# RoPE's half swap from DMA copies to a TensorE permutation, and the weight sums from bf16 to fp32

## The reference

```
h  = modulate(rms_norm(x, g_attn), sh_a, sc_a)
q_w, k_w, v_w, q_n, k_n, v_n, q_g, k_g, v_g = split_mixer_inputs(h @ w_in, qk_g)   # rms norm per head of q and k
q_w, k_w = apply_rope(q_w, cos, sin), apply_rope(k_w, cos, sin)
q_g, k_g = apply_rope(q_g, cos, sin), apply_rope(k_g, cos, sin)

def apply_rope(x, cos, sin):
    x1, x2 = x[..., :half], x[..., half:]
    return concatenate([x1 * cos - x2 * sin, x2 * cos + x1 * sin], axis=-1)
```

## Time and profile before

| what | value |
|---|---|
| median of three runs | 1783.89 us |
| the profiled execution's own time | 1784.84 us |
| its span, first to last instruction | 1783.0 us |
| VectorE / ScalarE / GpSimd busy | 959.8 / 663.4 / 784.2 us |
| dense matmuls (L890), three forms | 581.1 + 378.1 + 310.9 us |
| DMA, mean over the span | 100 GB/s |

### The profile page before, as it was taken

How to read it: one execution, slowest core, us unless ns; L and a number is a source line. 1 busy time by engine, 2 the same in 40 slices (tenths; PEclk the granted TensorE clock), 3 DMA queues, 4 the chain that set the end, 5 groups by cost and what they waited for, 6 DMA issues and landing times.

```text
span 1783.0 us, 27785 instructions
## 1 busy us (share of the span) xinstructions
PE 1665.5 (93%) x10959; PEld 1229.3 (69%) x10959; DVE 959.8 (54%) x1715; ACT 663.4 (37%) x1218; POOL 784.2 (44%) x576
## 2 busy tenths in 40 slices
PE   7999988977989999999899998997887999999998
PEld 3688877866856678666776687886776645645646
DVE  4434498894458851686418844457995612112112
ACT  3222367774243320243013113226875354053130
POOL 2234345652523553345414342551334557468363
PEclk9999999999989999999999998998999899999999
DMA  9355542313124523345225422554003224333332
GB/s 317 48 129 141 131 128 79 90 49 83 36 82 132 149 65 95 95 130 154 59 84 172 148 71 48 144 132 109 16 1 89 78 71 119 94 96 105 83 83 83
DMA packets 317279, 179.11 MB, mean 100 GB/s; under 512 B 88526, under 2 KB 310494, under 8 KB 317150
## 3 DMA queue, kind: packets, MB, share of 16 engines
q1 hardware_dynamic: 284542, 143.63, 30.7%
q10 hardware_dynamic: 32608, 33.71, 6.1%
HBM read 158.97 MB, written 2.83 MB: 91 GB/s over the span
## 4 chain that ended last, share of the span: by engine, by line
PE 60%; DVE 5%; POOL 2%; issue 2%; ACT 2%; SPq 1%; DMA 0%; DVEq 0%; ACTq 0%; POOLq 0%
PE acc L890 55%; PE small L1161 1%; DVE act L1612 1%; DVE stat L1774 1%; DVE prob_t L1788 1%; POOL split_w L656 1%; DVE scaled_ffn L1626 1%; PE side L1071 0%; POOL pair_w L762 0%; PE mod_ps L987 0%; ACT prob_t L1413 0%; DVE o_sum L1800 0%; PE side L880 0%; SPq L546 0%; ACT prob L1391 0%
## 5 line engine op out<-in xcount | busy, mean ns | idle before, releaser
L890 PE MATMUL acc<-act,pair_w 128*128 128x512 f16 x3168 | 581.1, 345 | 6.7 <-ACT act L1277 4.2
L890 PEld LDWEIGHTS acc<-act,pair_w 128*128 128x128 f16 x3168 | 307.6, 98 | 270.1 <-DVE act L1612 9.4
L890 PE MATMUL acc<-act,split_w 128*128 128x512 f32 (+1 forms) x1920 | 378.1, 355 | 9.1 <-DVE act L1874 2.9
L890 PEld LDWEIGHTS acc<-act,split_w 128*128 128x128 f32 x1920 | 307.6, 190 | 61.8 <-DVE act L1874 4.8
L890 PE MATMUL acc<-hidden,split_w 128*128 128x512 f32 (+1 forms) x1584 | 310.9, 358 | 10.6 <-issue 6.3
L890 PEld LDWEIGHTS acc<-hidden,split_w 128*128 128x128 f32 x1584 | 261.3, 189 | 57.7 <-issue 7.1
L653 POOL TENSOR_SCALAR split_w<-raw_w 128x1024 fp32r<-128x1024 f32 (+1 forms) x120 | 126.0, 1050 | 396.3 <-PE acc L890 301.8
L656 POOL TENSOR_TENSOR split_w<-raw_w,split_w 128x1024 fp32r<-128x1024 f32 (+1 forms) x120 | 278.3, 2319 | 10.0
L759 POOL TENSOR_SCALAR pair_raw<-pair_raw,weight_scale 128x1024 f32<-128x1024 f32 x88 | 105.8, 1202 | 356.8 <-ACT pair_w L1462 356.8
L1937 DVE SCALAR_TENSOR_TENSOR mod_acc<-mod_chunk,silu_c,mod_acc 128x256 f32<-128x256 f32 x280 | 228.1, 857 | 4.0
L1637 DVE SCALAR_TENSOR_TENSOR x_t<-acc,mod,x_t 128x512 f32<-128x512 f32 x96 | 60.3, 658 | 254.1 <-PE acc L890 253.6
(11 more groups left out here) (188 smaller groups left out, 1831.8 us busy)
## 6 DMA issues: line engine op xcount, KB each, us to landing
mod_chunk<-in_w_mod ACTq DMA_DIRECT2D x28, 1024.0 KB, 5.4
pair_raw<-in_w_gate SPq DMA_DIRECT2D x44, 512.0 KB, 4.1
pair_raw<-in_w_up SPq DMA_DIRECT2D x44, 512.0 KB, 5.5
raw_w<-in_w_in SPq DMA_DIRECT2D x64, 256.0 KB, 3.7
raw_w<-in_w_down SPq DMA_DIRECT2D x32, 512.0 KB, 3.8
raw_w<-in_w_mod SPq DMA_DIRECT2D x24, 512.0 KB, 4.1
mod_start<-in_w_mod SPq DMA_DIRECT2D x8, 1024.0 KB, 12.1
ks<-q_split SPq DMA_DIRECT2D x64, 96.0 KB, 2.2
```

What stands on the lines that cost most here:

```text
L890: mm = pe.matmul(acc[slot][:, a:b], weights[:, part == 2, k, :], moving[:, part == 1, k, a:b], start=(k == 0 and part == 0), stop=(k == n ...
```

## The change

The swap becomes a matmul. A constant `swap`, 128 by 128 in fp32, with a one at (p, p ^ 32), is loaded with the other constants. A new function `after_norm(j - 3)` stands in TensorE's loop between the dense work of unit j and `after_copy(j - 1)`: it waits for `q_normed`, from the second on also for `q_sin_ready` of the one before, and writes the swapped tile into the PSUM bank `small` by one fp32 matmul of 512 columns. `rotate` reads it there. `swap_halves` and its DMAs are gone, and with them ScalarE's wait for `q_normed` at that place.

`rotate(m - 4)` moves ahead of `take_values` and `inverse` on VectorE. The weight sums use `ones` and `weight_sum` in fp32 instead of the bf16 pair.

```diff
-            for dst, src in ((pair_ones, k_pairs), (cos, k_cos), (sin, k_sin)):
+            for dst, src in ((pair_ones, k_pairs), (swap, k_swap), (cos, k_cos), (sin, k_sin)):
...
-            pool.memset(ones16[:, :], 1.0).then_inc(filled, 1)
...
-                if n == 0:
-                    pe.wait_ge(filled, 3)
...
-                high = weight_sum[:, 2 * f:2 * f + 2].bitcast(BF16)[:, 1:4:2]
-                pe.matmul(mod_ps[:, 0:2], ones16[:, :], high, start=True, stop=True).then_inc(weight_ps, 1)
+                pe.matmul(mod_ps[:, 0:2], ones[:, :], weight_sum[:, 2 * f:2 * f + 2], start=True, stop=True).then_inc(weight_ps, 1)
...
+                def after_norm(j):
+                    if not 0 <= j < 16 or QKV[j][0] not in "qk":
+                        return
+                    i = l * N_ROPE + rope_before(j)
+                    pe.wait_ge(q_normed, l * N_QK + qk_before(j) + 1)
+                    if i >= 1:
+                        pe.wait_ge(q_sin_ready, i)
+                    pe.matmul(small[:, 0:LAT], swap[:, :], q_n[i % 2][:, :], start=True, stop=True).then_inc(q_swapped, 1)
...
+                    after_norm(j - 3)
                     after_copy(j - 1)
...
-                def swap_halves(j):
-                    if not 0 <= j < 16 or QKV[j][0] not in "qk":
-                        return
-                    r = l * N_ROPE + rope_before(j)
-                    sc.wait_ge(q_normed, l * N_QK + qk_before(j) + 1)
-                    if r:
-                        sc.wait_ge(q_ready, r)
-                    for p in range(0, P, 32):
-                        sc.dma_start(q_sin[p:p + 32, :], q_n[r % 2][p ^ 32:(p ^ 32) + 32, :]).then_inc(swap_in, 16)
...
-                    swap_halves(j - 3)
...
-                    ve.wait_ge(swap_in, 64 * (r + 1))
-                    ve.tensor_tensor(q_sin[:, :], q_sin[:, :], sin[:, :], ALU.mult).then_inc(q_sin_ready, 1)
+                    ve.wait_ge(q_swapped, r + 1)
+                    if r:
+                        ve.wait_ge(q_ready, r)
+                    ve.tensor_tensor(q_sin[:, :], small[:, 0:LAT], sin[:, :], ALU.mult).then_inc(q_sin_ready, 1)
...
+                    rotate(m - 4)
+                    take_values(m - 2)
                     inverse(m - 2)
-                    take_values(m - 2)
-                    rotate(m - 4)
...
+    swap = (p[:, None] == (p[None, :] ^ 32)).astype(f)
```

More of the change, by code:

```diff
@@ L206, in trunk @@
 def trunk(nc, x, c, ctx, c_ctx, w_mod, b_mod, norm_attn, norm_ffn, w_in, qk_norm, sink, rpb, w_out,
-          w_gate, w_up, w_down, k_ident, k_pairs, k_cos, k_sin, k_window, k_columns, out):
+          w_gate, w_up, w_down, k_ident, k_pairs, k_swap, k_cos, k_sin, k_window, k_columns, out):
     inv_dram = nc.dram_tensor("inv_rows", [2, 2, TOK], F32, kind="Internal").ap()
@@ L230, in trunk @@
         pair_ones = place("pair_ones", [P, P], F32)
+        swap = place("swap", [P, P], F32)
         ones = place("ones", [P, P], F32)
-        ones16 = place("ones16", [P, P], BF16)
         cos = place("cos", [P, LAT], F32)
@@ L362, in trunk @@
         qkv_copied, q_sq, q_ssq, q_root, q_inv = sem("qkv_copied"), sem("q_sq"), sem("q_ssq"), sem("q_root"), sem("q_inv")
-        q_normed, swap_in, q_cos_ready, q_sin_ready, q_ready = (
-            sem("q_normed"), sem("swap_in"), sem("q_cos_ready"), sem("q_sin_ready"), sem("q_ready"))
+        q_normed, q_swapped, q_cos_ready, q_sin_ready, q_ready = (
+            sem("q_normed"), sem("q_swapped"), sem("q_cos_ready"), sem("q_sin_ready"), sem("q_ready"))
         v_ps, v_ready, v_hi = sem("v_ps"), sem("v_ready"), sem("v_hi")
@@ L1974 @@
 N_VECS = 4 + 3 * DEPTH
-N_CONST = 6
+N_CONST = 7
 def shape_constants():
@@ L1997, in shape_constants @@
         columns[:, VARIANT[cb]] = np.where(ok, 0, NEG)
-    return {"k_ident": ident, "k_pairs": pairs, "k_cos": cos, "k_sin": sin.astype(f),
+    return {"k_ident": ident, "k_pairs": pairs, "k_swap": swap, "k_cos": cos, "k_sin": sin.astype(f),
             "k_window": window, "k_columns": columns}
```

## The result

The changed kernel takes 1798.32 us (median of 5 runs, 1795.54 to 1804.24), the kernel before, timed beside it, 1783.89 (5 runs, 1781.23 to 1788.44). The ratio is 1.0083 with a 95% interval of 1.0057 to 1.0107: slower by 14.8 us, give or take 4.5. I had forecast 1805.2, which is 21.3 us more, with a range of 1797.5 to 1811.0. The ratios of this document leave out three single executions that took far longer than all others (9469.82 us in experiment 2, 1935.27 in experiment 6, 2418.45 of the kernel before beside experiments 5 to 8).

What follows compares the result with a forecast made beforehand. TensorE, busy 93% and full in the projections and gate and up, was taken to bound the kernel. Swaps 14.2, sums 6.6 and waits 0.5 add 21.3 us to 1783.89, giving 1805.2 us, range 1797.5 to 1811 for 8 in 10.

Steps and rivals of the forecast that it cites:

- The swap matmuls: Projections, both layers: 16 fp32 matmuls of 512 columns at 0.89 us, 14.2 us (13.9 to 17.0), on TensorE's path.
- The weight sums: 44 sums, 22 in a layer: fp32 instead of bf16 adds 0.15 us each, 6.6 us (4.0 to 7.9).
- these stand in a stream that is 60.00 of 60.00 busy, so this is on the path too: Weight sums: with TensorE full in gate and up of layer 1, their 6.6 us counts wholly in the time.
- the sums vanish: Rival: fp32 sums vanish between big matmuls, leaving 14.2 + 0.5, 1798.6 us; one part cheap, either one, 0.19.
- The new waits: TensorE waits for normed tiles, units 4 and 6 in layer 1: 0.5 us (0 to 4.8).
- What is free: Projections: dropped copy DMAs, ScalarE's wait, PSUM read, later reciprocal, constant load and attention's start cost or gain nothing.
- The sum: Whole kernel: 14.2 + 6.6 + 0.5 = 21.3 us more, 1805.2 us from the median.
- signs of being right: Swap 0.87 to 0.9 us; projections full, about 7 us longer; VectorE waits for TensorE, not DMA; gate-and-up period 10.5.
- The swap waits in full: Rival: lateness of units 4 and 6 in layer 1 paid fully, 4.8 not 0.5 us, 1809.5; chance 0.14.
- A swap costs one record: Rival: a swap takes one record of 0.435 us, not two, 1798.0 us; one part cheap, either one, 0.19.
- Faster: Rival: VectorE's chain paces the projections, so 44.3 us of waiting come back, 1760.9 us; chance 0.04.
- The clock: Attention's start: later arrival may shift low-clock stretches a few us either way; widens the range, no chance of its own.

Runs made afterwards that it cites:

- experiment 2: Kernel before with only the weight sums in fp32: 1785.7 us, ratio 1.0000 (0.9989 to 1.0012).
- experiment 6: Kernel before with the weight sums in fp32 in layer 0 only: 1784.55 us, ratio 0.9998 (0.9985 to 1.0011).
- experiments 5 to 8: Kernel before with fp32 sums and moved late modulation, fp32 sums layer 0 only, layer 1 only; changed kernel with doubled swap: 1780.76, 1784.55, 1783.82, 1813.82 us.
- experiment 5: Kernel before with late modulation moved off hidden tiles 7 and 15 and weight sums in fp32: 1780.76 us, ratio 0.9978 (0.9965 to 0.9992).
- experiments 1 and 4: Changed kernel with sums back in bf16: 1800.73 us, ratio 1.0089; changed kernel with late modulation moved off the chunk's last tile: 1797.87 us, ratio 1.0068.
- experiment 9: Changed kernel with VectorE's old order (inverse, take_values, then rotate): 1799.91 us, ratio 1.0080 (1.0058 to 1.0101).
- experiment 8: Changed kernel with every swap matmul issued twice: 1813.82 us, ratio 1.0161 (1.0139 to 1.0182).
- experiments 6 and 7: Kernel before with fp32 weight sums in layer 0 only: 1784.55 us, ratio 0.9998; in layer 1 only: 1783.82 us, ratio 1.0000.
- experiment 3: Kernel before with late modulation moved off the chunk's last tile (from tiles 7, 15 to 6, 14): 1777.83 us, ratio 0.9959 (0.9946 to 0.9972).

## Why the prediction came out as it did

**The swap matmuls: right.** Forecast 0.89 us each and 14.2 in all, all of it on the path. Measured 0.86 us between starts, 13.8 in all, 6.80 or 6.94 in layer 0, and 13.74 when doubled. The Trainium skill's Perfetto Trace Analysis, section Engine Utilization, read as the cost of a whole matmul, would have had half of it; the swap runs in two records, each at that rate, and the trace is what decides.

**The weight sums: the step that failed.** Two things are to be told apart. The size: 0.12 us each (0.115 as a stage's mean, 0.92 for 8) and not 0.15, so 5.0 and not 6.6 us gross. I had taken the 0.21 us between starts from a train of squares for a lone sum; the lone one takes 0.14 (1583.67 to 1583.81), against 0.03 in bf16. And the step "these stand in a stream that is 60.00 of 60.00 busy, so this is on the path too". That row is of layer 1. In layer 0 the gate and up units are as full, but the down projections behind them contain pauses that depend on how VectorE stands to GpSimd, and there the 2.3 us come back as 1.20 and, by the execution, 1.72 to 4.20. A stage being full says that its own length grows by the edit, which it did; it does not say that the sum over the stages does. The net price in the kernel before is 0.0 (experiment 2, with 2 us to either side), and 2.9 to 3.4 with the pause gone (experiment 5). My rival "the sums vanish", 1798.6, came nearest to the time and for a reason that was not its own: they don't vanish between the big matmuls, they are paid and given back elsewhere.

**The new waits: too small.** Forecast 0.5 us, bounds 0 and 4.8. The projection of layer 1 is longer by 10.55, 9.49, 10.13 and 9.03 us in four profiles with the swap and the new order (experiments 1 and 4 are the last two), of which 6.8 is the swap itself, so 2.2 to 3.7 remain; but the sums alone and the kernel before again have 1.8 and 2.1 there too, without any swap matmul, so measured from those profiles the change adds only 0.1 to 2.0 beside its 6.8. What is the change's own among these I can bound and not settle: the waits for `q_n` are 1.0 and 1.6 us in two executions, and a clock fall of about 1.6 us stands behind the wait in one of them. The forecast had the mechanism (unit 4's inverse behind SyncE's eight issues) and the place, and priced VectorE's side of it at its undisturbed durations. Unit 6, the larger lateness in its rows, waited 0 us in the first profile of the kernel after and 0.48 in the second.

**What is free: nearly right.** VectorE's wait moved from DMA to TensorE as told, and TensorE waited for nothing there but the tiles of the paragraph above. Turning `rotate` ahead is neither gain nor loss in the time (experiment 9), though it moves the rotation's addition beside GpSimd's split.

**The sum.** Forecast 14.2 + 6.6 + 0.5 = 21.3. With the pause out of the way the chip gives 20.0; 13.8 for the swap and 3.4 for the sums leave 2.8 for waits, with 3 us of uncertainty on the 20.0 and on the 3.4 alike. The forecast's terms are then 0.4 and 3.2 us too high and 2.3 too low, which leaves it 1.3 above the 20.0. In the kernel as it stands it is 14.4, and the 5.6 that are left are the pause and the clock behind it. That the time fell into the range is so partly luck: the giveback, which the forecast lacks, took most of the 7.7 us between its middle and its lower end. Of its signs of being right, the swap's 0.86 us, the moved wait of VectorE and the period of 10.50 us came out; TensorE at 25.00 of 25.00 and about 7 us more in a projection hold in layer 0 and not in layer 1.

**The rivals.** "The swap waits in full" is refuted by the waits, 1.0 and 1.6 and not 4.8 us. "A swap costs one record" by experiment 8. "Faster" by all of them. "The clock" stands: between two profiles of the same kernel its falls move and stages change by 1 to 2.5 us.

**What stays open.** What the sums cost in time to better than 3 us. How much the clock adds to the giveback, 1.7 us in one profile and -0.8 in the other. And the contention of VectorE and GpSimd: experiments 6 and 7 show that layer 0's sums remove 2.4 us of it and experiment 3 that the pause goes when the work is elsewhere, but no run here moved GpSimd's split alone, so it is read from rows that recur in ten profiles and not shown by a test of its own.

## What to carry to other kernels

Price an edit on the bounding engine by starts in the trace, and then look through all later stages for pauses of that engine: a pause can take in as much time as the edit adds (here 3 to 5 us against the 5.0 of the sums), and then neither the edit's price nor its being on the path tells the total. To see the true price, take the pause away from both kernels and compare again; here it turned 14.4 into 20.0 us, and gave, as its own result, the fastest version, 1777.83 us. Profile each kernel more than once: stages of one kernel differed by up to 2.5 us between two executions. Work that an engine does off the path should not stand in its queue ahead of an instruction that frees the bound engine's buffers, above all at the end of a chunk.

## What the runs showed of the hardware

A VectorE instruction whose operands lie in SBUF is held up beside GpSimd's work on weights in the rows of this case, and by how much hangs on which of the two starts first. The seven late instructions of experiment 3, with GpSimd idle beside them, take 3.61 us where the same seven took 9.55 and 11.05 above:

```profile
843.19 3.61 DVE L1937 SCALAR_TENSOR_TENSOR mod_acc<-mod_chunk,silu_c,mod_acc 128x256 f32<-128x256 f32 x7
```

Each of the held ones among the seven in those two profiles ends 0.27 or 0.28 us after GpSimd's instruction beside it does, so they look held until it has ended rather than slowed in proportion. It goes the other way too. In the first chunk GpSimd's split before, and then after:

```profile
650.41 1.07 POOL L653 TENSOR_SCALAR split_w<-raw_w 128x1024 fp32r<-128x1024 f32 x1 [2.89 <-PE acc L890]
```

```profile
660.31 2.94 POOL L652 TENSOR_SCALAR split_w<-raw_w 128x1024 fp32r<-128x1024 f32 x1 [3.00 <-PE acc L889]
```

Before, the next of VectorE's instructions starts 0.08 us behind the split and takes 1.26 us; after, it starts 0.02 ahead of it, VectorE's last five run at 0.47 us each, and the split is the one that takes 2.94 instead of 1.07. So 0.1 us of phase decides which of the two engines waits. It isn't exact to a hundredth: the instruction at 850.79 started 0.01 ahead of the split and was held all the same.

The rotation's addition of 128 x 512 fp32 stands in layer 0 of the kernel after right behind a multiplication of the same shape:

```profile
107.63 0.69 DVE L1737 TENSOR_TENSOR q_sin<-small,sin 128x512 f32<-128x512 f32 x1 [6.03 <-PE small L1003]
108.35 2.61 DVE L1741 TENSOR_TENSOR q_raw<-q_raw,q_sin 128x512 f32<-128x512 f32 x1
```

The first reads one operand from PSUM and takes 0.69 us; the second has both in SBUF and takes 2.61, beside GpSimd's

```profile
108.02 2.39 POOL L655 TENSOR_TENSOR split_w<-raw_w,split_w 128x1024 fp32r<-128x1024 f32 x1
```

In layer 1 its twin at 1148.00 takes 2.62 beside

```profile
1147.67 2.41 POOL L655 TENSOR_TENSOR split_w<-raw_w,split_w 128x1024 fp32r<-128x1024 f32 x1
```

and 0.69 in experiment 9, at 1151.45, when GpSimd is idle. Both long ones end 0.54 or 0.55 us after GpSimd's instruction beside them. The Trainium skill's GPSIMD Engine Reference, section Specifications, says that GpSimd shares its SBUF interfaces with VectorE, with contention for VectorE instructions that have two SBUF inputs. These rows agree: the operand in PSUM is spared and the other is not. The first instruction of the late modulation, 0.35 or 1.21 us, has a single tensor in SBUF and a scalar and is stretched as well, which that sentence would allow only if it ran in one of the modes that it also names; no run here shows whether it did.
